# Expert jobs in the order of their experts, one weight load for each expert, and a combine in one-pass matmuls

## The chip, the core and the metric

One NeuronCore of a Trainium2 chip runs one program. Its engines each have a queue of instructions of their own: TensorE (PE in the profile, with its weight loads as PEld), VectorE (DVE), ScalarE (ACT), GpSimd (POOL) and SyncE (SP), which here issues nearly all weight DMAs. Engines wait for one another through semaphores only. The metric is the device time of one execution in microseconds (us). The kernel before takes 1644.32 us (median of three runs, 1644.28 to 1646.38).

## The reference, cut to what matters

Two transformer blocks follow one another on 256 tokens of width 1024. The change touches the mixture of experts at the end of the second (32 experts, 4 chosen for each token, so 1024 assignments), in float32:

```python
logits = (ht @ w_router + b_router).astype(jnp.float32)
top_vals, top_idx = lax.top_k(logits, TOP_K)
gates = jax.nn.softmax(top_vals, axis=-1)
...
def expert_block(args):
    xblk, e = args
    gu = xblk @ w_gate_up[e] + b_gate_up[e]
    gate = jnp.minimum(gu[:, :D_EXPERT], SWIGLU_LIMIT)
    up = jnp.clip(gu[:, D_EXPERT:], -SWIGLU_LIMIT, SWIGLU_LIMIT)
    act = gate * jax.nn.sigmoid(SWIGLU_ALPHA * gate) * (up + 1)
    return act @ w_down[e] + b_down[e]
...
y = jnp.zeros((T + 1, D), h.dtype).at[row_tok].add(row_gate[:, None].astype(h.dtype) * yb)
```

`w_gate_up[e]` is 1024 x 2048 (8 MB), `w_down[e]` 1024 x 1024 (4 MB). With the reference's inputs expert 8 is chosen by 72 tokens and every other expert by 57 or fewer.

## The kernel before

**Jobs.** The experts' work is cut into jobs of up to 64 tokens (`SLOTS`) of one expert. The first 32 jobs are the 32 experts; an expert with more than 64 tokens gets further jobs, which stand behind all others. Here that is one, so there are 33 jobs. VectorE finds the tables of the jobs (expert, token positions, gates) on wide tiles of 16 x 32 numbers (`choose`), beside the first job's matmuls.

**One job on TensorE.** `gather` picks the job's token rows out of `x_n` with a 0/1 matrix `picks` (L1826). `bias` starts the four PSUM banks 0 to 3 (L1836, fp32r, 64 partitions deep: high and low parts of the biases). `gate_up` adds the products with eight weight slots in four pairs (L1849); a pair is 16 matmul instructions with a weight tile of 64 columns each, even chunks into the upper 64 rows of a bank and odd chunks into the lower 64 rows. A float32 matmul of the program is two instructions in the trace, an fp32r matmul or a transposition one. `turn_act` transposes the activation (L1861), `down` multiplies by four weight slots (L1901), `turn_mix` transposes a matrix that holds the gate at each token's slot (L1891), and `combine` spreads the result over the 256 tokens with it (L1873, float32, 64 deep). ScalarE and VectorE fetch the two half sums out of the banks (`lo_rows` and `swap`, L769, L754; L1384, L1357), form the activation on 64 partitions x 1024 (L1390 to L1400), and add the combined rows to `h` (L1376).

**Pipeline.** A turn of the loop holds gate/up of one job (`m + 2`) and, at its end, down of the job before (`m + 1`); combine follows one more turn later. So the activation of a job is made while the next work runs on TensorE.

**Loads.** Twelve slots of 1 MB hold the weights of one job: six of `ring`, six of `ring_b`. SyncE reloads a pair of gate/up slots when TensorE has used it (`gu_used`), and a down slot likewise (`d_used`), for the next job's expert, which it reads from `job_expert`. Every job loads its 12 MB, also the second job of an expert. There is no second set of slots.

## Time and profile before

| | |
|---|---|
| Median of the runs | 1644.32 us |
| The profiled execution's own time | 1646.69 us |
| Its span, first to last instruction | 1644.9 us |
| PE / PEld / DVE / ACT busy | 1540.6 / 859.6 / 674.7 / 383.3 us |
| Mean granted TensorE clock | 0.957 |
| HBM read | 492.36 MB |

The experts' part runs from about 620 us to the end. The profile is read from the page to the windows, and from there to the order of time: the windows say which engines are full, the timeline how long each piece of a turn holds TensorE. A piece's length is taken from the start of one row to the start of the next, since matmul ends overlap.

### The profile page before, as it was taken

How to read it: one execution, taken by the hardware profiler on the slowest of the kernel's cores; microseconds unless marked ns; L12 is line 12 of the kernel's file. 1: busy time of each engine (PE TensorE's matmuls, PEld its weight loads, DVE VectorE, ACT ScalarE, POOL GpSimd, SP SyncE). 2: the span in 40 equal slices, each digit the busy share in tenths (PEclk: the TensorE clock that was granted, in tenths of full speed). 3: DMA queues.
4: the chain of work that ended last, by engine and by line, in shares of the span. 5: the costliest groups of instructions: out<-in, count | busy, mean ns of one | idle time of the engine just before them, and what ended most of it. 6: DMA issues, size and time to landing. Idle time of an engine off the chain costs nothing.

```text
span 1644.9 us, 21236 instructions
## 1 busy us (share of the span) xinstructions
PE 1540.6 (94%) x7730; PEld 859.6 (52%) x7730; DVE 674.7 (41%) x1053; ACT 383.3 (23%) x607; POOL 87.9 (5%) x106
## 2 busy tenths in 40 slices
PE   6999797999968688999999999999999999999995
PEld 5768564899956645344443444444444444344431
DVE  2134424766743425433334334343343343433433
ACT  0222002444312301212213122122131221221212
POOL 2000001322312000000000000000000000000000
PEclk9999797999979787999999999999999999999997
DMA  6332233555523434899999999999999999999993
GB/s 237 132 137 103 102 103 124 169 191 180 170 94 134 179 114 161 328 414 421 422 421 421 421 421 421 421 422 421 422 422 421 421 421 422 422 421 422 421 380 128
DMA packets 106812, 493.82 MB, mean 300 GB/s; under 512 B 10255, under 2 KB 34496, under 8 KB 56032
## 3 DMA queue, kind: packets, MB, share of 16 engines
q1 hardware_dynamic: 103136, 489.85, 74.3%
q10 hardware_dynamic: 3648, 3.59, 0.7%
q8 instruction: 19, 0.31, 0.1%
q14 instruction: 9, 0.07, 0.0%
HBM read 492.36 MB, written 1.05 MB: 300 GB/s over the span
## 4 chain that ended last, share of the span: by engine, by line
issue 64%; PE 31%; DVE 3%; POOL 1%; ACT 1%; DVEq 0%; POOLq 0%; ACTq 0%
PE bank L1480 8%; PE bank L1665 7%; PE bank L1488 6%; PE bank L1677 4%; PE bank L1634 2%; PE bank L1470 1%; PE bank L1777 0%; PE bank L1739 0%; POOL rstd L451 0%; PE bank L1767 0%; DVE u_lo L1119 0%; DVE h_lo L1078 0%; PE bank L1607 0%; PE bank L1544 0%; ACT score L712 0%
## 5 line engine op out<-in xcount | busy, mean ns | idle before, releaser
L1849 PE MATMUL bank<-ring,x_T 128*64 128x512 f32 x1584 | 365.3, 604 | 0.0
L1901 PE MATMUL bank<-ring_b,act_T 128*64 128x512 f32 x1056 | 234.2, 596 | 0.0
L1849 PEld LDWEIGHTS bank<-ring,x_T 128*64 128x64 f32 x1584 | 106.0, 138 | 212.6 <-issue 210.5
L1376 DVE TENSOR_TENSOR h<-h,bank 128x512 f32<-128x512 f32 x128 | 82.2, 684 | 309.3 <-PE bank L1873 296.2
L769 ACT ACTIVATE lo_rows<-bank 64x512 f32<-64x512 f32 x132 | 67.7, 589 | 533.9 <-PE bank L1849 533.9
L1901 PEld LDWEIGHTS bank<-ring_b,act_T 128*64 128x64 f32 x1056 | 73.0, 137 | 137.9 <-issue 137.9
L1826 PEld LDWEIGHTS bank<-picks,x_n 128*128 128x128 f32 x1056 | 123.6, 196 | 27.1 <-issue 27.1
L1384 DVE TENSOR_TENSOR gate<-bank,lo_rows 64x512 f32<-64x512 f32 x66 | 42.3, 678 | 222.9 <-ACT lo_rows L769 222.9
L1826 PE MATMUL bank<-picks,x_n 128*128 128x64 f32 x1056 | 128.2, 281 | 2.3 <-DVE picks L1287 2.3
L1849 PE MATMUL bank<-ring_b,x_T 128*64 128x512 f32 x528 | 120.6, 598 | 0.0
L1480 PE MATMUL bank<-x_nT,ring 128*128 128x256 f32 x512 | 113.8, 385 | 0.8 <-DVE x_nT L878 0.8
L1480 PEld LDWEIGHTS bank<-x_nT,ring 128*128 128x128 f32 x512 | 98.4, 193 | 15.4 <-DVE x_nT L878 1.2
L1665 PE MATMUL bank<-h_hi,ff_hi 128*128 128x256 f32 x352 | 100.5, 285 | 1.9 <-DVE ff_lo L1093 1.9
L1665 PE MATMUL bank<-h_lo,ff_hi 128*128 128x256 f32 x352 | 100.1, 285 | 0.0
L1665 PE MATMUL bank<-h_hi,ff_lo 128*128 128x256 f32 x352 | 100.1, 284 | 0.0
L1357 DVE TENSOR_TENSOR y<-bank,swap 128x512 f32<-128x512 f32 x66 | 45.6, 692 | 80.3 <-ACT swap L755 67.9
L451 POOL TENSOR_TENSOR rstd<-msq,neg_half 128x2 f32<-128x2 f32 (+2 forms) x10 | 8.5, 858 | 1256.7 <-DVE msq L858 1213.4
L1873 PE MATMUL bank<-y,mix_w 64*128 64x512 f32 x248 | 70.0, 641 | 0.0
L1665 PEld LDWEIGHTS bank<-h_hi,ff_hi 128*128 128x128 f32 x352 | 68.2, 194 | 3.4 <-DVE ff_lo L1093 3.0
L1665 PEld LDWEIGHTS bank<-h_lo,ff_hi 128*128 128x128 f32 x352 | 68.2, 194 | 0.4
L1665 PEld LDWEIGHTS bank<-h_hi,ff_lo 128*128 128x128 f32 x352 | 68.1, 193 | 0.0
L1849 PEld LDWEIGHTS bank<-ring_b,x_T 128*64 128x64 f32 x528 | 35.0, 136 | 59.4 <-issue 57.3
(363 smaller groups left out, 1688.8 us busy)
## 6 DMA issues: line engine op xcount, KB each, us to landing
ring<-in_w_gate_up SPq DMA_DIRECT2D x198, 1024.0 KB, 11.4
ring_b<-in_w_down SPq DMA_DIRECT2D x132, 1024.0 KB, 11.3
ring_b<-in_w_gate_up SPq DMA_DIRECT2D x66, 1024.0 KB, 8.4
ring<-in_w_in SPq DMA_DIRECT2D x22, 1024.0 KB, 7.3
ring<-in_w_ffn_in SPq DMA_DIRECT2D x22, 1024.0 KB, 5.1
ring<-in_w_ffn_out SPq DMA_DIRECT2D x11, 1024.0 KB, 4.9
ring<-in_w_out SPq DMA_DIRECT2D x8, 1024.0 KB, 5.4
ring<-in_w_branch_sb SPq DMA_DIRECT2D x2, 1024.0 KB, 5.1
```

Source lines behind the costliest of these rows:

```text
L769: act.activation(t.lo_rows[0:SLOTS, n, :], g.banks[n][SLOTS:, :], ACT.Copy).then_inc(s.lo_rows_ready, 1)
L1357: dve.tensor_tensor(t.y[:, c, :], g.banks[first + c][:], t.swap[:, c, :], ALU.add).then_inc(s.y_summed, 1)
L1376: dve.tensor_tensor(t.h[:, b, cols], t.h[:, b, cols], g.banks[4 + b][:], ALU.add).then_inc(s.added, 1)
L1384: dve.tensor_tensor(dst, g.banks[n][0:SLOTS, :], t.lo_rows[0:SLOTS, n, :], ALU.add).then_inc(s.summed, 1)
L1480: ins = pe.matmul(bank[:, j * T:(j + 1) * T], wk[:, f * P:(f + 1) * P], src[:, k, :], start=(k == 0), stop=(k == len(weights) - 1))
L1488: ins = pe.matmul(bank[:, 0:n], src[:, k, b * P:(b + 1) * P], wk[:, c0:c0 + n], start=(k == 0), stop=(k == len(weights) - 1))
L1665: ins = pe.matmul(bank[:, f * T:(f + 1) * T], wt[:, k, f * P:(f + 1) * P], ht[:, k, :], start=(k == 0 and part == 0), stop=(k == KT - 1 an ...
L1677: ins = pe.matmul(banks[2 * b + c][:], ut[:, q, k, b * P:(b + 1) * P], wt[:, k, 512 * c:512 * c + 512], start=False, stop=last, skip_group ...
L1826: ins = pe.matmul(banks[6][:, f * SLOTS:(f + 1) * SLOTS], t.h_n[:, b, f * P:(f + 1) * P], t.picks[:, b, :], start=(b == 0), stop=(b == 1))
L1849: ins = pe.matmul(banks[n][rows, :], t.x_T[:, c, :], job_slot(g, c)[:, 512 * n:512 * n + 512], start=False, stop=(pair == 3), skip_group_c ...
L1873: ins = pe.matmul(banks[outs + b][:], t.mix_w[rows, b * P:(b + 1) * P], t.y[rows, c, :], start=start, stop=True, skip_group_check=True)
L1901: ins = pe.matmul(banks[outs + n][rows, :], t.act_T[:, 2 * c + i, :], job_slot(g, GU + c)[:, D * i + 512 * n:D * i + 512 * n + 512], start ...
```

## The change

- **Tables.** The jobs are sorted by expert. The number of tokens of each expert comes from a matmul, running sums over experts from matmuls with triangles (`before4`, `upto4`), and the tables of positions, gates and experts from small matmuls with the matrix `job_sel` (job m belongs to expert e).
- **Loads.** SyncE's loop runs over the 31 further experts, not over jobs. It reads `job_last[e]`, the number of the last job of expert e, and reloads a slot when that job has used it.
- **Order.** Gate/up and down of a job stand in one turn. The last pair of gate/up counts bank by bank (`gu_full`). Combine of the job before stands between pairs 1 and 2 and between pairs 2 and 3.
- **Activation.** The two halves of 512 columns lie on the two halves of the partitions, so it is formed on 128 x 512, with the last product written in transposed column order for four 128 x 128 transpositions.
- **Combine.** The gates are no longer in the matrix (`spread` is 0/1); the result is multiplied by the gate (`slot_gate`) and split in a high and a low fp32r part. `bias` and `combine` alternate between the two halves of 64 rows.

```diff
+    sp.wait_ge(s.jobs_ready, 1)
+    with sp.Fori(0, E - 1) as m:
+        last = sp.value_load(t.job_last[0:1, bass.ds(m, 1)], min_val=0, max_val=E + OVER - 1)
         for c in range(GU):
-            if c % 2 == 0:
-                sp.wait_ge(s.gu_used, nth(m, o, 4, c // 2 + 1))
-            load_gu(e, c)
+            pair = c // 2
+            if c % 2 == 0 and pair < PAIRS - 1:
+                sp.wait_ge(s.gu_used, last * (PAIRS - 1) + (pair + 1))
+            elif c % 2 == 0:
+                sp.wait_ge(s.gu_full, last * 4 + 4)
+            load_gu(m + 1, c)
         for c in range(DN):
-            sp.wait_ge(s.d_used, nth(m, o, 4, c - 3))
-            load_down(e, c)
+            sp.wait_ge(s.d_used, last * DN + (c + 1))
+            load_down(m + 1, c)
...
         for n in range(4):
-            ins = pe.matmul(banks[n][:], t.bias_sel[0:64, :], t.bias_hl[0:64, 512 * n:512 * n + 512], start=True,
-                            stop=False, skip_group_check=True)
+            n = n // 2 + 2 * (n % 2)
+            rows, cols = slice(SLOTS * (n // 2), SLOTS * (n // 2) + SLOTS), slice(512 * (n % 2), 512 * (n % 2) + 512)
+            ins = pe.matmul(banks[n][:], t.bias_sel[rows, :], t.bias_hl[rows, cols], start=True, stop=False,
+                            skip_group_check=True)
...
+    def turn_weights(m, o):
+
+        pe.wait_ge(s.mix_in_ready, nth(m, o, 3, 3))
         if m is not None or o > 0:
+            pe.wait_ge(s.act_T_ready, nth(m, o, 1, 0))
+        for b in range(NB):
+            pe.transpose(banks[7][:, b * P:(b + 1) * P], t.mix_in[:, b, :], t.ident[:])
+        for b in range(NB):
+            ins = pe.matmul(banks[7][:, T:T + 1], t.mix_in[:, b, :], t.gate_col[:, b:b + 1], start=(b == 0),
+                            stop=(b == 1))
+        ins.then_inc(s.weights_turned, 1)
...
+        for part in (t.y_hi, t.y_lo):
+            for c in range(2):
+                rows = slice(SLOTS * c, SLOTS * c + SLOTS)
+                ins = pe.matmul(banks[outs + c][:], t.spread[rows, b * P:(b + 1) * P], part[rows, :],
+                                start=(part is t.y_hi), stop=(part is t.y_lo), skip_group_check=True)
         ins.then_inc(s.combined, 1)
...
+    def crossed_gate_up(m, o):
+
         if m is not None or o > 0:
             act.wait_ge(s.summed, nth(m, o, 4, 0))
         for n in range(4):
+            there, here = (slice(SLOTS, P), slice(0, SLOTS)) if n % 2 == 0 else (slice(0, SLOTS), slice(SLOTS, P))
+            act.wait_ge(s.gu_full, nth(m, o, 4, n + 1))
+            act.activation(t.cross[here, n // 2, :], g.banks[n][there, :], ACT.Copy).then_inc(s.crossed, 1)
...
+    next_job(None, 1)
+    add_combined(None, -1)
     swiglu(None, 0)
-    weights(None, 0)
-    next_job(None, 2)
-    add_combined(None, -1)
-    swiglu(None, 1)
```

**TensorE, one turn of the job loop**, in the order of its queue. `y` and `mix_w` belong to combine, `picks` to gather, `act` to turn_act. Before:

```order
561 L1849 MATMUL bank<-ring,x_T 64x512 x8
562 L1855 REGISTER_ALU
563 L1857 REGISTER_ALU
564 L1861 MATMUL bank<-ident,act 128x64 x8
565 L1849 MATMUL bank<-ring,x_T 64x512 x8
566 L1867 ISA
567 L1873 MATMUL bank<-y,mix_w 128x512 x2
568 L1849 MATMUL bank<-ring,x_T 64x512 x8
569 L1870 REGISTER_ALU
570 L1873 MATMUL bank<-y,mix_w 128x512 x2
```

After, from the first combine of the turn to its end:

```order
551 L1860 MATMUL bank<-y_hi,spread 128x512 x2
552 L1860 MATMUL bank<-y_lo,spread 128x512 x2
557 L1842 ISA
558 L1846 MATMUL bank<-ident,mix_in 128x128 x2
559 L1848 MATMUL bank<-gate_col,mix_in 128x1 x2
561 L1825 MATMUL bank<-ring_b,x_T 64x512 x8
562 L1796 ISA
563 L1799 MATMUL bank<-picks,x_n 128x64 x16
564 L1835 REGISTER_ALU
565 L1837 MATMUL bank<-ident,act 128x128 x4
566 L1876 REGISTER_ALU
567 L1882 MATMUL bank<-ring_b,act_T 64x512 x16
```

The transpositions of the activation have moved from behind the next job's first pair to the place right ahead of down of their own job, with only the gather between them and the last gate/up pair. `L1876` is down's wait for the transposed activation.

**TensorE, the first job**, after:

```order
534 L1869 MATMUL bank<-b_down,gate_T 128x512 x2
535 L1825 MATMUL bank<-ring_b,x_T 64x512 x8
536 L1799 MATMUL bank<-picks,x_n 128x64 x16
537 L1869 MATMUL bank<-b_down,gate_T 128x512 x2
538 L1837 MATMUL bank<-ident,act 128x128 x4
539 L1882 MATMUL bank<-ring_b,act_T 64x512 x16
```

Before, the two groups of `b_down` matmuls stood between gate/up pairs of the second job. Now the second of them stands between the first job's last pair and its transpositions, and VectorE's sums of it (`add_combined(None, -1)`) stand ahead of the first job's activation.

## Rows read from the trace of the kernel before

**Rows 1.** The page: chain that ended last by engine; DMA issues of `w_down`.

```profile
issue 64%; PE 31%; DVE 3%; POOL 1%; ACT 1%; DVEq 0%; POOLq 0%; ACTq 0%
...
ring_b<-in_w_down SPq DMA_DIRECT2D x132, 1024.0 KB, 11.3
```

**Rows 2.** Windows: length, busy of PE, PEld, DVE, ACT, POOL, clock, DMA share, GB/s.

```profile
620.00:650.00 30.00, 25.22 (x102) 14.85 (x102) 20.28 (x58) 4.37 (x5) 0.00 (x0) 0.64 0.27 100
...
1000.00:1100.00 100.00, 100.00 (x514) 43.44 (x512) 36.35 (x61) 20.47 (x36) 0.00 (x0) 1.00 1.01 422
```

**Rows 3.** Timeline of PE in one turn: start, length, line, operation, shapes, count.

```profile
1001.01 1.13 PE L1873 MATMUL bank<-y,mix_w 64*128 64x512 f32 x4
1002.07 3.65 PE L1849 MATMUL bank<-ring,x_T 128*64 128x512 f32 x16
...
1006.72 3.79 PE L1826 MATMUL bank<-picks,x_n 128*128 128x64 f32 x32
1010.43 3.65 PE L1849 MATMUL bank<-ring_b,x_T 128*64 128x512 f32 x16
1014.02 0.44 PE L1891 MATMUL bank<-ident,mix_in 128*128 128x128 f32 x2
1014.38 7.09 PE L1901 MATMUL bank<-ring_b,act_T 128*64 128x512 f32 x32
1021.40 1.19 PE L1836 MATMUL bank<-bias_hl,bias_sel 64*128 64x512 f32 x4
1022.53 3.65 PE L1849 MATMUL bank<-ring,x_T 128*64 128x512 f32 x16
1026.11 1.17 PE L1861 MATMUL bank<-ident,act 64*128 64x64 f32 x8
...
1030.80 1.13 PE L1873 MATMUL bank<-y,mix_w 64*128 64x512 f32 x4
```

**Rows 4.** Timeline of PE, float32 matmuls of the full 128 x 128 tile.

```profile
601.41 3.60 PE L1488 MATMUL bank<-ring,y_pool 128*128 128x512 f32 x8
```

**Rows 5.** Timeline of ACT and DVE, the steps of one activation (and its transposed copy).

```profile
1593.14 0.60 ACT L760 ACTIVATE act_T<-bank 128x512 f32<-128x512 f32 x1 [3.28 <-PE bank L1861]
...
1606.10 2.05 ACT L769 ACTIVATE lo_rows<-bank 64x512 f32<-64x512 f32 x4 [12.36 <-PE bank L1849]
...
1606.72 1.28 DVE L1384 TENSOR_TENSOR gate<-bank,lo_rows 64x512 f32<-64x512 f32 x2 [3.00 <-ACT lo_rows L769]
...
1608.04 0.69 DVE L1390 TENSOR_SCALAR gate<-gate 64x1024 f32<-64x1024 f32 x1
...
1610.76 1.22 DVE L1398 SCALAR_TENSOR_TENSOR act<-act,gate 64x1024 f32<-64x1024 f32 x1
```

**Rows 6.** DMA issues (median us to landing): at 780 to 900, at 1500 to 1610, and an FFN load.

```profile
ring<-in_w_gate_up SPq DMA_DIRECT2D x24, 1024.0 KB, 10.7
...
ring<-in_w_gate_up SPq DMA_DIRECT2D x18, 1024.0 KB, 12.7
...
ring<-in_w_ffn_out SPq DMA_DIRECT2D x11, 1024.0 KB, 4.9
```

**Rows 7.** Timeline of DVE and PE from the routing to the first turn of the loop.

```profile
621.83 0.58 DVE L1267 TENSOR_REDUCE mask<-one_hot 128x64 f32<-128x256 f32 x1
...
627.55 7.06 PE L1826 MATMUL bank<-picks,x_n 128*128 128x64 f32 x32 [2.31 <-DVE picks L1287]
...
636.54 12.89 PE L1849 MATMUL bank<-ring,x_T 128*64 128x512 f32 x48
...
660.65 1.20 PE L1836 MATMUL bank<-bias_hl,bias_sel 64*128 64x512 f32 x4 [3.93 <-DVE act L1384]
...
693.82 1.20 PE L1836 MATMUL bank<-bias_hl,bias_sel 64*128 64x512 f32 x4
```

**Rows 8.** Timeline: PE behind the loop's last down, DVE's last additions to `h`.

```profile
1613.38 1.14 PE L1861 MATMUL bank<-ident,act 64*128 64x64 f32 x8
...
1634.39 1.41 DVE L1431 TENSOR_TENSOR h<-h,bank 128x512 f32<-128x512 f32 x2 [0.16 <-DVE h L1431]
```

More of the change, by code:

```diff
@@ L359, in load_down @@
     def load_down(e, c):
[L360 to L363 removed]
+        sp.dma_start(job_slot(g, GU + c), down[e, c // 2, c % 2]).then_inc(s.job_landed(GU + c), 16)
     for c, back in ((0, 6), (1, 5)):
@@ L1883, in down_bias, with down @@
+    def down_bias(b):
+        if b == 1:
+            pe.wait_ge(s.added, 2)
+        for c in range(2):
+            ins = pe.matmul(banks[4 + c][:], t.gate_T[0:E, b * P:(b + 1) * P], t.b_down[0:E, 512 * c:512 * c + 512],
                             start=True, stop=True)
         ins.then_inc(s.combined, 1)
-    def turn_mix(m, o):
-        pe.wait_ge(s.mix_in_ready, nth(m, o, 2, 2))
+    def down(m, o, e):
         pe.wait_ge(s.act_T_ready, nth(m, o, 1, 1))
-        for b in range(NB):
-            ins = pe.transpose(banks[7][:, b * P:(b + 1) * P], t.mix_in[:, b, :], t.ident[:])
-        ins.then_inc(s.weights_turned, 1)
@@ L1925, in tensor_program @@
-    gate_up(None, 1, 3)
-    turn_mix(None, 0)
-    pe.wait_ge(s.added, 2 * NB)
-    down(None, 0, 4)
-    def job_turn(m, final=False):
-        bias(m, 2)
-        gate_up(m, 2, 0)
-        turn_act(m, 1)
-        gate_up(m, 2, 1)
-        combine(m, 0, 0, 4)
-        gate_up(m, 2, 2)
-        combine(m, 0, 1, 4)
-        if not final:
-            gather(m, 3)
-        gate_up(m, 2, 3)
-        turn_mix(m, 1)
-        pe.wait_ge(s.added, nth(m, 1, 4, 4))
-        down(m, 1, 4)
-    pe.wait_ge(s.jobs_ready, 1)
@@ L1947, in tensor_program @@
-    more = pe.value_load(t.job_count[0:1, 0:1], min_val=E - 3, max_val=E + OVER - 3)
+    pe.wait_ge(s.over_ready, 1)
+    for n, sums in enumerate((t.before4, t.upto4)):
+        ins = pe.matmul(banks[5][:, n:n + 1], sums[0:E, :], t.over[0:E, :], start=True, stop=True)
+    ins.then_inc(s.starts_made, 1)
+    pe.wait_ge(s.bias_ready, 2)
+    bias(None, 0)
+    gate_up(None, 0, 0, 0)
+    bank = open_bank(r2, "gT")
+    pe.wait_ge(s.gates_ready, 1)
+    for b in range(NB):
+        ins = pe.transpose(bank[0:E, b * P:(b + 1) * P], t.gate_e[:, b, :], t.ident[:])
@@ new lines, in tensor_program @@
+    ins.then_inc(s.filled2, 1)
+    gate_up(None, 0, 0, 1)
+    pe.wait_ge(s.sel_ready, 1)
+    pe.wait_ge(s.pos_T_ready, 1)
+    pe.wait_ge(*r2.drained("gT"))
+    for b in range(NB):
+        toks, pos, gate = (slice(c0, c0 + n) for c0, n in ((b * P, P), (b * JOBS, JOBS), (128 + b * JOBS, JOBS)))
+        pe.matmul(banks[4][:, pos], t.pos_T[0:E, toks], t.job_sel[0:E, :], start=True, stop=False)
+        pe.matmul(banks[4][:, pos], t.back[0:E, :], t.block[0:E, :], start=False, stop=True)
+        pe.matmul(banks[4][:, gate], t.gate_T[0:E, toks], t.job_sel[0:E, :], start=True, stop=True)
@@ new lines, in tensor_program @@
+    pe.matmul(banks[4][0:1, 256:256 + JOBS], t.part32[0:E, :], t.job_sel[0:E, :], start=True, stop=True)
+    pe.matmul(banks[4][0:1, 320:320 + E], t.span[0:E, 1:2], t.ident[0:E, 0:E], start=True,
+              stop=True).then_inc(s.tables_made, 1)
+    turn_weights(None, 0)
+    gate_up(None, 0, 0, 2)
+    pe.wait_ge(s.b_down_in, 16)
+    pe.wait_ge(s.jobs_ready, 1)
+    down_bias(0)
+    gate_up(None, 0, 0, 3)
+    gather(None, 1)
+    down_bias(1)
+    turn_act(None, 0)
+    down(None, 0, 0)
@@ new lines, in job_turn @@
+    def job_turn(m, final=False):
+        e = pe.value_load(t.job_expert[0:1, bass.ds(m + 1, 1)], min_val=0, max_val=E - 1)
+        bias(m, 1)
+        gate_up(m, 1, e, 0)
+        gate_up(m, 1, e, 1)
+        combine(m, 0, 0)
+        gate_up(m, 1, e, 2)
+        combine(m, 0, 1)
+        turn_weights(m, 1)
+        gate_up(m, 1, e, 3)
+        if not final:
+            gather(m, 2)
+        turn_act(m, 1)
+        down(m, 1, e)
+    more = pe.value_load(t.job_count[0:1, 0:1], min_val=E - 2, max_val=E + OVER - 2)
```

490 lines of the change are left out of this document (224 added, 266 removed).

## The prediction, made before the changed kernel ran

> **What bounds the kernel now.** I read the page first. Its chain of what ended last calls 64% of the span "issue", time in which TensorE waited for nothing that the profile shows, so the experts' part is one unbroken stream of matmuls [rows 1]. The windows confirm it: in 1000 to 1100 us PE is busy for 100.00 of 100 us at a granted clock of 1.00 (the 2.4 GHz level). They show a second thing: the DMA engines are full as well (share 1.01, 422 GB/s) [rows 2]. Both resources are at their end and only one can set the pace. A turn takes 1030.80 - 1001.01 = 29.79 us on PE [rows 3]. The 12 MB of a job (12.58 million bytes) at 421 to 422 GB/s take 29.85, call it 29.87. The time to landing decides: a load lands 10.7 us after its issue early in the loop and 12.7 late in it [rows 6]. The queue grows very slowly, by under 0.1 us a turn, and a landed slot still waits over 10 us for its use. So PE sets the pace, and DMA stands 0.3% behind it. There are 132 / 4 = 33 jobs [rows 1].
>
> **A turn, piece by piece.** By starts in [rows 3]: combine 1.06, twice; a gate/up pair 3.59, four times; gather 3.71; turn_mix 0.36; down 7.02; bias 1.13; turn_act takes what is left of 29.79, 1.10. Down has 32 instructions and a pair 16: 16 more cost 3.43, so 0.16 of each stretch is the change from one form of weight tile to another (for that, the Trainium skill, TensorEngine Tiling (Array Packing), "Key Properties", says that a change of mode drains the engine; the trace agrees, and what it costs here is the 0.16).
>
> - **Bias and combine.** Four bias instructions cost 1.13 - 0.16 = 0.97, 0.24 each, one after another in the same rows. The two float32 matmuls of a combine are four instructions in 1.06 although one alone takes 0.43 (8 in 3.60 [rows 4]): the two halves of rows run side by side. After, bias and combine are four one-pass instructions each that alternate between the halves. Taken side by side: 2 x 0.24 + 0.16 = 0.64. No row shows fp32r in alternating halves, so the bounds are 0.64 and 1.13 (the bias row as it is); I take 0.64, since the halves are what the combine row shows to be shared. Saved: 0.49 and 2 x 0.42.
> - **Gate/up** is unchanged, 4 x 3.59, less one change of form between pairs 0 and 1: 14.20.
> - **turn_weights** is turn_mix plus two matmuls of one column, four instructions that each load 128 weight columns; a gather instruction, which is bound by that load, costs (3.71 - 0.16) / 32 = 0.11. So 0.36 + 0.44 = 0.80.
> - **Gather** 3.55, without the change of form at its end.
> - **turn_act and the wait behind it.** Four transpositions at 0.12 to 0.16 each (bounded by turn_act's 8 in 1.10 and turn_mix's 2 in 0.36), about 0.6 with the drain. Then down needs `act_T`, which ScalarE copies in 0.60 [rows 5]; with two hand-overs of 0.05 and its being behind the copy of `x_T`, PE stands still for about 0.8. Before, this copy was hidden behind a gate/up pair. Together 1.4.
> - **Down** 7.02. A read of `job_expert` is added at the head of each turn; the read of `job_count` before the first turn left down at its full pace and cost nothing visible, and I take 0.
>
> Sum: 0.64 + 1.28 + 14.20 + 0.80 + 3.55 + 1.4 + 7.02 = **28.9 us** a turn (28.8 to 29.3), against 29.79.
>
> **The wait that is added.** The transpositions wait for the activation of the same job. Behind the last gate/up pair only the gather, 3.55, covers it. From the start of that pair: banks 0 to 3 are full at about 1.07, 1.92, 2.78 and 3.64. ScalarE's copies take 0.59, VectorE's additions 0.64 to 0.68, a limit on 128 x 512 half of 0.69 plus overhead, 0.43, a product half of 1.22 plus overhead, 0.67 [rows 5]. The additions end at 2.4, 3.3, 4.35 and 5.0, the second limit at 5.5, the two products at 6.2 and 6.9. PE would reach the transpositions at 3.59 + 3.55 = 7.14. The chain fits with 0.2 to spare: cover is thin, and each 0.1 more on that chain beyond it costs 3 us over 32 turns. The sum over `h`, the new split in high and low part and the job's tables lie beside gate/up: from the end of down they need about 3.4 us, and combine comes 7.7 us later.
>
> **Loads after.** They would be 32 x 12 MB, but the saved load does not shorten DMA by its 29.9 us: during expert 8's first job no slot is given back, DMA runs empty, and it starts again in job 9. From there it is always full: 23 experts at 29.87. The first pair is free 4.2 us into job 9's turn. The second-last pair of the last expert lands 22 x 29.87 + 6 x 2.49 + 2.4 later (2.4 is the 4.9 us of an unqueued load [rows 6] less its 2.49 of transfer), 678.6 us after job 9's start, and 20.7 us of the turn remain: 699.3. PE alone needs 24 x 28.9 = 693.6. So DMA takes over shortly before the end, and the part from job 9 on takes 699 for every turn below 29.14. This is a floor; the first nine jobs are PE's.
>
> **Before the loop** [rows 7]. The mask is there at 622.4; the rank matmuls no longer wait for the gates, so gather starts at about 625.1 instead of 627.55. It takes 7.06 as now, the clock in this stretch being granted at 0.64 on average [rows 2], two small matmuls 0.9, bias 1.2: the first pair at 634.2 instead of 636.54. It costs 5.9 with the slow clock. Then 0.4 (gates turned), 3.6, tables 2.1 (16 instructions at 0.11 and changes of form), 0.8, 3.6, `b_down` 1.9, 3.6, gather 3.7, `b_down` 1.9: 661.7. Here VectorE begins the two last additions of `b_down` and only then the activation: 1.4 + 2.6 + 0.9 + 1.4 = 6.4 with PE idle, twice the 3.93 that [rows 7] shows now. After that gap the clock falls again, as it did at 660.65; transpositions and copy 1.8, down 9. The loop starts with job 1 at **679**, against 693.82 with job 2. So 32 turns remain instead of 31.
>
> **The end.** Job 9 starts at 679 + 8 x 28.9 = 910.2, and the last down ends 699.3 later, plus 1.8 for a slow clock in the last turn, where no gather covers the activation: 1611.3. Before, it is 1613.38 [rows 8]; there a second down and two more combines follow, and the last addition to `h` ends at 1635.80, 9.1 before the end. Now there follow half sums and split 3.4, combine about 0.9, additions 2.8: 7.1, and the same 9.1. Span 1611.3 + 16.2 = **1627.5**, 17.4 less than 1644.9. The profiled execution took 1646.69 where the median is 1644.32; I take the difference from the median and get **1627 us**, 1.05% faster.
>
> **Rivals.**
> - **The halves do not run side by side in fp32r.** Then bias and both combines stay at 1.13 and a turn is 28.9 + 3 x 0.49 = 30.4. 32 turns from 679 end at 1651, the span at 1669: **1668 us**, slower. It speaks for it that no row shows it, against it that the float32 combine does it in the same tiles. The point of decision is a piece length of about 0.9. By TensorE: Matmul & The Clock Gate, Part 3, of the Trainium skill, a weight load overlaps running matmuls only in other rows, and combine loads its low part's weights under the high part: that would give the same lengthening by another way. The bias row, at 0.24 per one-pass instruction in the same rows, speaks against it.
> - **The activation outlasts the gather.** If the hand-overs or the product with strided output take 0.5 to 1.0 more in all, a turn is 29.2 to 29.7: span 1637 to 1653, typically **1643**.
> - **Loads slower.** `w_down` is now read in pieces of 8 KB at twice the distance. If those four of twelve loads take 5% more, an expert takes 30.4 and the floor from job 9 rises by 11: **1638**.
> - **The part before the loop is better hidden** (clock stays up, no gap of 6.4): 5 less, **1621**.
>
> **How the numbers follow.** Forecast 1619 to 1636: 0.62. Activation longer 0.16; loads slower 0.07; halves one after another 0.08; still faster 0.07. A difference of about 0.2% (3.3 us) is what a measurement can tell from none. Faster by more holds the forecast, the last, and most of the two middle ones: 0.80. Within 0.2%: 0.07. Slower 0.13, mostly the first rival. The range leaves out that rival and the tails: 1616 to 1650.
>
> **What would show it.** In the profile after: starts of a turn 28.9 apart before job 9; bias and combine pieces near 0.64, or 1.13 if the first rival holds; one gap of PE of 0.8 a turn before down, released by ScalarE's `act_T`, and none before the transpositions; DMA below full in job 8's turn, then full, with landing times growing by about 1 us a turn, and PE waiting for slots only in the last turns; a gap of 6 us before the first job's transpositions. I am wrong if a turn is not within 28.7 to 29.3, or if waits for loads appear early.

## The result, and the profile after

The changed kernel takes 1648.35 us (median of 15 runs, 1645.69 to 1652.40), the kernel before beside it 1644.35 us (15 runs, 1642.03 to 1648.43). The ratio is 1.0021, with a 95% interval of 1.0011 to 1.0031. The forecast was 1627 us. So the change that was to save 17 us costs 4. The profiled execution of after took 1650.08 us, its span is 1648.3 us, its mean granted TensorE clock 0.950, PE was busy for 1504.2 us (1540.6 before), and 479.77 MB were read (492.36 before). TensorE has 36 us less work and ends later.

Here is the same view as [rows 3], TensorE in one turn of the loop: start, length, line, operation, count, and in brackets the idle time ahead and what ended it.

```profile
705.29 0.74 PE L1812 MATMUL bank<-bias_hl,bias_sel 64*128 64x512 f32 x4
705.96 7.09 PE L1825 MATMUL bank<-ring,x_T 128*64 128x512 f32 x32
712.98 0.50 PE L1860 MATMUL bank<-y_hi,spread 64*128 64x512 f32 x2
...
713.64 3.65 PE L1825 MATMUL bank<-ring,x_T 128*64 128x512 f32 x16
717.23 0.50 PE L1860 MATMUL bank<-y_hi,spread 64*128 64x512 f32 x2
...
717.89 0.44 PE L1846 MATMUL bank<-ident,mix_in 128*128 128x128 f32 x2
...
718.60 3.65 PE L1825 MATMUL bank<-ring_b,x_T 128*64 128x512 f32 x16
722.18 3.79 PE L1799 MATMUL bank<-picks,x_n 128*128 128x64 f32 x32
726.20 0.65 PE L1837 MATMUL bank<-ident,act 128*128 128x128 f32 x4 [0.24 <-DVE act L1376]
727.73 7.09 PE L1882 MATMUL bank<-ring_b,act_T 128*64 128x512 f32 x32 [0.88 <-ACT act_T L781]
734.75 0.74 PE L1812 MATMUL bank<-bias_hl,bias_sel 64*128 64x512 f32 x4
```

This turn takes 734.75 - 705.29 = 29.46 us, 0.33 less than before and 0.57 more than forecast. Bias takes 0.67 and each combine 0.66: those gains are there. But TensorE now stands still twice in every turn, 0.24 us ahead of the transpositions (waiting for VectorE's `act`) and 0.88 us ahead of down (waiting for ScalarE's `act_T`). In [rows 3] it never did.

VectorE on the activation of that job, to be held beside [rows 5], and ScalarE's copy of `act_T` behind the transpositions:

```profile
722.39 1.41 DVE L1360 TENSOR_TENSOR up<-bank,cross 64x512 f32<-64x512 f32 x2
723.83 0.43 DVE L1371 TENSOR_SCALAR up<-up 128x512 f32<-128x512 f32 x1
724.29 0.69 DVE L1373 TENSOR_TENSOR gate<-gate,sig 128x512 f32<-128x512 f32 x1
725.02 1.05 DVE L1376 SCALAR_TENSOR_TENSOR act<-up,gate 128x512 f32<-128x512 f32 x1
...
726.89 0.60 ACT L781 ACTIVATE act_T<-bank 128x512 f32<-128x512 f32 x1 [0.29 <-PE bank L1837]
```

The last product, written in transposed column order, takes 1.05 us where the product of the same shape above it takes 0.69. The chain ends at 726.07, 7.47 us after the last pair's start at 718.60.

The second finding is not in the usual turn but in every fourth. The windows (length, busy time of PE, PEld, DVE, ACT, POOL, granted clock, DMA share, GB/s) at the end of such a turn, where down starts at 875.00:

```profile
871.00:875.00 4.00, 2.89 (x25) 2.54 (x24) 2.24 (x4) 1.19 (x2) 0.00 (x0) 1.00 1.01 422
875.00:878.40 3.40, 3.40 (x8) 1.15 (x10) 0.00 (x0) 0.00 (x0) 0.00 (x0) 0.50 1.02 424
878.40:882.00 3.60, 3.60 (x20) 1.43 (x18) 0.00 (x0) 0.00 (x0) 0.00 (x0) 1.00 1.01 419
```

TensorE came out of the gather, two idle stretches and four transpositions (2.89 us busy of 4.00). For the first part of down the granted clock is then 0.50, the 1.2 GHz level: 8 matmuls in 3.40 us, against 20 in the 3.60 behind it. Such a turn takes 31.12 us instead of 29.45. There are seven of them among the 31 turns from 675.83 to 1600.53, always four turns (119.5 us) apart, and an eighth fall comes in the last turn's down. The kernel before had none in this part; its window from 700 to 1590 us:

```profile
700.00:1590.00 890.00, 890.00 (x4484) 376.17 (x4482) 336.22 (x565) 204.46 (x360) 0.00 (x0) 1.00 1.01 421
```

The loads, from the page (issues, KB each, median us to landing), beside [rows 1, 6]:

```profile
ring<-in_w_gate_up SPq DMA_DIRECT2D x192, 1024.0 KB, 9.6
ring_b<-in_w_down SPq DMA_DIRECT2D x128, 1024.0 KB, 8.2
```

A `w_down` load lands sooner than before (11.3), and no PE instruction in the loop waits for a load. The windows of the trace show DMA at a share of 1.01 up to 890 us, at 0.00 from 895 to 915 us, and at 1.00 again from 920 us on: it rests once, in expert 8's first job, as foreseen.

**The account.** From the start of job 1 to the end of the last down the forecast gave 932.3 us; after takes 1631.55 - 675.83 = 955.7. Of the 23.4 in between, 31 turns at 29.45 instead of 28.9 make 17.1, the seven falls 7 x 1.67 = 11.7, the last turn (31.0 where 28.9 and 1.8 were counted) 0.3; against this, the 5.7 us by which the loads were to hold back a faster TensorE at the end did not come. The loop starts 3.2 earlier than forecast, the tail is 0.5 longer (16.75 against 16.2): 23.4 - 3.2 + 0.5 = 20.7, and the span is 20.8 above 1627.5.

### The profile page after: what moved, and what is told of

The parts are those of the page before. It is cut to its first block, busy times and chain, and to the rows that moved or that the text cites. A ratio compares the mean times of both kernels' runs of the same rounds, so it can differ in the third digit from the quotient of the medians.

```text
span 1648.3 us, 21328 instructions
## 1 busy us (share of the span) xinstructions
PE 1504.2 (91%) x7752; PEld 861.7 (52%) x7753; DVE 659.7 (40%) x1103; ACT 372.9 (23%) x608; POOL 89.9 (5%) x117
## 3 DMA queue, kind: packets, MB, share of 16 engines
HBM read 479.77 MB, written 1.05 MB: 292 GB/s over the span
## 4 chain that ended last, share of the span: by engine, by line
issue 64%; PE 31%; DVE 3%; POOL 1%; ACT 1%; DVEq 0%; POOLq 0%; ACTq 0%
PE bank L1456 8%; PE bank L1641 7%; PE bank L1464 6%; PE bank L1653 4%; PE bank L1610 2%; PE bank L1446 1%; PE bank L1753 0%; PE bank L1715 0%; POOL rstd L434 0%; PE bank L1743 0%; DVE u_lo L1104 0%; DVE h_lo L1063 0%; PE bank L1583 0%; PE bank L1588 0%; PE bank L1520 0%
## 5 line engine op out<-in xcount | busy, mean ns | idle before, releaser
L1825 PE MATMUL bank<-ring,x_T 128*64 128x512 f32 x1584 | 356.5, 599 | 0.0
L1882 PE MATMUL bank<-ring_b,act_T 128*64 128x512 f32 x1056 | 248.3, 624 | 28.7 <-ACT act_T L781 28.7
L1319 DVE TENSOR_TENSOR y_sum<-bank,y_cross 64x512 f32<-64x512 f32 x66 | 45.5, 689 | 328.9 <-ACT y_cross L740 327.8
L1882 PEld LDWEIGHTS bank<-ring_b,act_T 128*64 128x64 f32 x1056 | 88.7, 144 | 167.3 <-issue 166.2
L1456 PEld LDWEIGHTS bank<-x_nT,ring 128*128 128x128 f32 x512 | 96.9, 190 | 14.8 <-DVE x_nT L863 1.1
L754 ACT ACTIVATE spread<-bank 128x256 fp32r<-128x256 f32 x33 | 12.6, 383 | 353.9 <-PE bank L1848 333.6
L764 ACT ACTIVATE cross<-bank 64x512 f32<-64x512 f32 x132 | 78.0, 591 | 41.5 <-PE bank L1825 41.4
L740 ACT ACTIVATE y_cross<-bank 64x512 f32<-64x512 f32 x33 | 19.6, 594 | 260.0 <-PE bank L1882 260.0
```

Of the source, the lines that this page charges most:

```text
L740: act.activation(t.y_cross[0:SLOTS, :], g.banks[4][SLOTS:, :], ACT.Copy).then_inc(s.y_crossed, 1)
L764: act.activation(t.cross[here, n // 2, :], g.banks[n][there, :], ACT.Copy).then_inc(s.crossed, 1)
L1319: dve.tensor_tensor(t.y_sum[rows, :], g.banks[4 + c][rows, :], t.y_cross[rows, :], ALU.add).then_inc(s.y_summed, 1)
L1456: ins = pe.matmul(bank[:, j * T:(j + 1) * T], wk[:, f * P:(f + 1) * P], src[:, k, :], start=(k == 0), stop=(k == len(weights) - 1))
L1825: ins = pe.matmul(banks[n][rows, :], t.x_T[:, c, :], job_slot(g, c)[:, 512 * n:512 * n + 512], start=False, stop=(pair == PAIRS - 1), skip ...
L1882: ins = pe.matmul(banks[4 + n][rows, :], t.act_T[:, k, SLOTS * (c // 2):SLOTS * (c // 2) + SLOTS], job_slot(g, GU + c)[:, D * i + 512 * n: ...
```

## The experiments

Each kernel is the changed kernel with the edit shown, unless another is named. They were timed beside the kernel before, whose median was 1644.09 (first four), 1644.0 (next four) and 1642.25 us (last four). The ratios are those recorded against the runs of the kernel before in the same session; they can differ by 0.15% from the quotient of the two medians.

### Which part of the excess is the chain

**e1_contiguous.**

```diff
-        dve.scalar_tensor_tensor(out=t.act[:].rearrange("s (k p) -> s p k", k=4),
-                                 in0=up[:].rearrange("s (p k) -> s p k", k=4), scalar=1.0,
-                                 in1=gate[:].rearrange("s (p k) -> s p k", k=4), op0=ALU.add,
-                                 op1=ALU.mult).then_inc(s.act_ready, 1)
+        dve.scalar_tensor_tensor(out=t.act[:], in0=up[:], scalar=1.0, in1=gate[:], op0=ALU.add,
+                                 op1=ALU.mult).then_inc(s.act_ready, 1)
...
-            ins = pe.transpose(banks[7][:, k * P:(k + 1) * P], t.act[:, k * P:(k + 1) * P], t.ident[:])
+            ins = pe.transpose(banks[7][:, k * P:(k + 1) * P], t.act[:, k:512:4], t.ident[:])
```

> The last product of the activation is written in its natural order (as before the change), and the transpositions read every fourth column. Theory A (TensorE sets the pace; turns of 29.46 us, of which every fourth is 1.67 longer because the clock falls to 1.2 GHz at the start of down): the product goes from 1.05 to about 0.67 us, the wait of 0.24 before the transpositions disappears, a usual turn is 29.22; about 7 us less in all, if the falls of the clock stay as often. Theory B (the loads set the pace: the mean turn of 29.83 equals 29.87, the time of 12 MB): the turn's pieces shorten in the same way, but the mean turn stays at 29.8 and the total within 2 us of the changed kernel.

Measured: 1630.99 us (1627.78 to 1632.16), ratio 0.9922 (0.9900 to 0.9943): 17 us below after, where theory A gave 7 with the falls left in, and no longer slower than before but 0.8% faster. The timeline of one turn, with the steps of TensorE and VectorE in it:

```profile
1011.37 3.79 PE L1797 MATMUL bank<-picks,x_n 128*128 128x64 f32 x32
...
1014.21 0.69 DVE L1376 SCALAR_TENSOR_TENSOR act<-up,gate 128x512 f32<-128x512 f32 x1
...
1015.03 0.74 PE L1835 MATMUL bank<-ident,act 128*128 128x128 f32 x4
...
1016.65 0.65 PE L1880 MATMUL bank<-ring_b,act_T 128*64 128x512 f32 x2 [0.88 <-ACT act_T L781]
```

The product takes 0.69 us, there is no idle time before the transpositions (3.66 from the gather's start, 4.02 in after), and the strided read costs TensorE 0.09 on the four transpositions. The turn is 29.19 us. The clock does not fall in any turn of the loop. So one edit, of the order in which one product is written and read, removes both the 0.27 a turn and the falls in the loop.

(Of the strided write, the Trainium skill, SBUF — State Buffer, "Door 1: The DMA port swizzle", says that each access that crosses to a new line of 16 bytes pays a penalty; it gives no size. The 1.05 against 0.69 agrees with it in direction.)

**e2_filler.**

```diff
         turn_act(m, 1)
+        pe.wait_ge(s.summed, nth(m, 1, 4, 4))
+        for n in range(FILL):
+            pe.matmul(banks[n][:], t.bias_sel[:, :], t.bias_hl[:, 0:512], start=True, stop=True,
+                      skip_group_check=True)
         down(m, 1, e)
```

with `FILL = 3`.

> Three useless one-pass matmuls of 512 columns stand between the transpositions and down, where TensorE waits 0.88 us for act_T; nothing is read from what they write. Theory A: they take 0.7 of time in which nothing ran, so a usual turn stays at 29.46, but the clock no longer falls in the loop: 8 x 1.67 = 13 us less than the changed kernel, 1635, and landing times of the loads grow over the loop (29.46 against 29.87). Theory B: no change, 1648, TensorE then waits for slots. Third theory (the clock falls because of the gather and the transpositions, not because of the gap): falls stay, 1648.

Measured: 1633.53 us (1629.45 to 1635.50), ratio 0.9931 (0.9909 to 0.9953). Three matmuls that nobody needs make the kernel 15 us faster than after:

```profile
1020.94 0.65 PE L1838 MATMUL bank<-ident,act 128*128 128x128 f32 x4 [0.24 <-DVE act L1377]
1021.35 0.95 PE L1940 MATMUL bank<-bias_hl,bias_sel 128*128 128x512 f32 x3
1022.28 7.09 PE L1883 MATMUL bank<-ring_b,act_T 128*64 128x512 f32 x32
```

The wait for `act` is still there, the wait for `act_T` is filled. No fall of the clock in the loop, and down starts 1.34 us after the start of the transpositions instead of 1.53. The turn is 29.27, where I had written 29.46. The gather and the transpositions stand as in after, so the third theory is out. This separates the falls from the chain: the chain is as long as in after, and what has changed is what TensorE does behind the transpositions.

**e11_fill_one** is the same with one matmul, `FILL = 1`.

> As e2_filler with one useless 128x512 matmul instead of three between the transpositions and the first matmul of down; its result is overwritten by the next bias. It ends about 0.6 us before act_T is there, so down still starts from standstill and the usual turn stays 29.45 us. Theory A (total idle time of a turn decides on the falls; 1.12 us before, 0.88 us now, and e1_contiguous with 0.88 us had none): no falls of the clock in the loop, 1633 to 1637 us. Theory B (a stretch without any wait before down is what prevents them): falls every 4th turn as before, 1646 to 1650 us.

Measured: 1631.36 us (1630.14 to 1635.32), ratio 0.9932 (0.9909 to 0.9954); the median is below my range, the ratio is that of e2_filler.

```profile
723.79 0.47 PE L1940 MATMUL bank<-bias_hl,bias_sel 128*128 128x512 f32 x1
724.08 0.60 ACT L782 ACTIVATE act_T<-bank 128x512 f32<-128x512 f32 x1 [0.29 <-PE bank L1838]
724.73 7.09 PE L1883 MATMUL bank<-ring_b,act_T 128*64 128x512 f32 x32 [0.46 <-ACT act_T L782]
```

One matmul is enough against the falls, with 0.46 us of wait left ahead of down. I was wrong on the turn: it is 29.26, not 29.45, since down starts 1.34 us after the transpositions (at 723.39) here too. Down's first matmul follows the end of ScalarE's copy by 0.24 us in after (727.49 to 727.73) and by 0.05 here (724.68 to 724.73). Whether the shorter stand does it, or that another instruction than a transposition stands ahead, no run tells.

### Is it the length of the chain or the strided access

**e9_contig_reclamp** is e1_contiguous with the chain made as long again by other means; `JOB_DVE_STEPS` becomes 3.

```diff
         own(dve.tensor_scalar(up[:], up[:], SWIGLU_LIMIT, -SWIGLU_LIMIT, ALU.min, ALU.max))
+        own(dve.tensor_scalar(up[:, 0:384], up[:, 0:384], SWIGLU_LIMIT, -SWIGLU_LIMIT, ALU.min, ALU.max))
```

> The product is written in natural order as in e1_contiguous (0.69 us instead of 1.05), but `up` is clamped a second time on 384 of its 512 columns ahead of it (about 0.35 us, changes no value), so that the activation chain is as long as in the changed kernel. Theory A (it is the length of the chain against the gather that costs, whatever makes it long): TensorE idle again about 0.25 us before the transpositions and 0.88 us behind them, usual turns 29.45 us, a fall of the clock about every 4th turn, 1645 to 1650 us. Theory C (the strided product itself does harm, by its accesses): turns 29.2 us, no falls, 1629 to 1633 us as e1_contiguous.

Measured: 1647.27 us (1643.66 to 1652.10), ratio 1.0025 (1.0011 to 1.0039). Nearly the whole gain of e1_contiguous is gone, so it was the length and not the access.

```profile
730.39 0.74 PE L1836 MATMUL bank<-ident,act 128*128 128x128 f32 x4 [0.27 <-DVE act L1377]
732.01 7.09 PE L1881 MATMUL bank<-ring_b,act_T 128*64 128x512 f32 x32 [0.88 <-ACT act_T L781]
```

But the parts differ from what I expected. The usual turn is 29.58 (the longer strided transpositions come on top of the wait), and the profiled execution has three falls in the loop, not seven, at 761, 1000 and 1031 us. It has slightly more idle time in a turn than after (1.15 against 1.12) and fewer falls. That execution is the slowest of the ten (1652.10 us); no other was traced.

**e10_reclamp** is after with a second clamp of all 512 columns.

> The changed kernel with a second clamp of `up` on all 512 columns (0.43 us and 0.03 to the next, changes no value), so that the chain is 0.46 us longer. Theory A (idle time in every turn makes the clock fall): TensorE idle 0.70 us before the transpositions, usual turns 29.91 us (14.7 us over all), and the falls come more often than every 4th turn: every 3rd gives 4 us more, every 2nd 13 us: 1667 to 1676 us. Theory D (the falls keep their own distance of about 119.5 us, whatever the idle time): 1663 us.

Measured: 1679.11 us (1677.06 to 1680.24), ratio 1.0214 (1.0194 to 1.0234), 31 us above after for 0.46 us of VectorE's time in a turn. The timeline at the transpositions and down of one turn, and a window at the start of another turn's down (columns as above):

```profile
728.26 0.65 PE L1838 MATMUL bank<-ident,act 128*128 128x128 f32 x4 [0.69 <-DVE act L1377]
729.79 8.46 PE L1883 MATMUL bank<-ring_b,act_T 128*64 128x512 f32 x32 [0.88 <-ACT act_T L781]
```

```profile
790.70:794.00 3.30, 3.02 (x8) 1.11 (x10) 0.00 (x0) 0.04 (x1) 0.00 (x0) 0.50 1.00 417
```

The usual turn is 29.91 as computed, and the clock falls in every second turn (31.53 us), in 16 of 31, with one pair of falls in neighbouring turns. So theory D, falls at a fixed distance of their own, is out, and more idle time at this place brought more falls. The 31 us are 14.7 from the chain, nine more falls at 1.62 for 14.6, and about 2 in the first job. The upper end of my range, 1676, was 3 us short.

### The gap before down

**e3_bias_in_gap** moves the next job's bias, which needs nothing of this one, to the place where TensorE waits for `act_T` (in the first job likewise).

```diff
-        bias(m, 1)
         gate_up(m, 1, e, 0)
...
         turn_act(m, 1)
+        if not final:
+            bias(m, 2)
         down(m, 1, e)
```

> The next job's bias matmuls (0.66 a turn) stand between the transpositions and down instead of at the head of the next turn. Theory A: they fill the gap, a usual turn is 28.8, and the clock falls no more; then DMA becomes the bound some turns after job 9 and the total is 1624 to 1630 against 1648. If the clock keeps falling every fourth turn: 13 us more, about 1638. Theory B: 1646 to 1648.

Measured: 1623.99 us (1622.32 to 1628.23), ratio 0.9878 (0.9860 to 0.9896). The timeline of TensorE in an early turn, from its transpositions to its down, and two pairs of a late one, and the window of the late turns:

```profile
726.93 0.65 PE L1837 MATMUL bank<-ident,act 128*128 128x128 f32 x4 [0.24 <-DVE act L1376]
727.51 0.73 PE L1812 MATMUL bank<-bias_hl,bias_sel 64*128 64x512 f32 x4
728.27 7.09 PE L1882 MATMUL bank<-ring_b,act_T 128*64 128x512 f32 x32
...
1282.05 3.65 PE L1825 MATMUL bank<-ring,x_T 128*64 128x512 f32 x16 [0.42 <-DMA ring<-in_w_gate_up]
...
1287.02 3.65 PE L1825 MATMUL bank<-ring,x_T 128*64 128x512 f32 x16 [0.65 <-DMA ring<-in_w_gate_up]
```

```profile
1211.00:1585.00 374.00, 357.64 (x1875) 157.58 (x1872) 135.33 (x259) 80.96 (x148) 0.00 (x0) 1.00 1.01 422
```

The turn is 28.45 us until about 1211 us (I had written 28.8: down also starts 0.19 sooner behind the transpositions, as in e2_filler), and no clock falls in it. From there TensorE waits for its loads in every turn, 1.07 us in the one shown, and a turn takes 29.83, the time of 12 MB. Here the floor of the prediction is seen at work. The late turns show one thing more. By the window TensorE stands for 374.00 - 357.64 = 16.4 us in 12.5 turns, 1.3 us a turn, more than the 1.12 of after, and the clock stayed at 1.00. These waits lie between long rows of gate/up matmuls, and only 0.24 us of them ahead of the transpositions. So it is not the sum of idle time in a turn that brings the falls.

### Are the loads the pace of after

A mean turn of after is (1600.53 - 675.83) / 31 = 29.83 us, the very time that DMA needs for 12 MB. That looks like a kernel bound by its loads.

**e4_half_loads.** From expert 1 on only the first half of each slot is loaded.

```diff
-            load_gu(m + 1, c)
+            sp.dma_start(job_slot(g, c)[:, 0:CW // 2],
+                         gate_up[m + 1, c][:, 0:CW // 2]).then_inc(s.job_landed(c), 16)
```

and likewise for `w_down`.

> From the second expert on only the first half of every weight slot is loaded (the other half keeps the first expert's numbers), so DMA needs half of its time; all matmuls stay. Theory A: the same time as the changed kernel, 1648, the same turns of 29.46 with every fourth 31.1. Theory B: the turns fall to TensorE's own work, all of them 29.46, and the total to about 1635.

Measured: 1651.72 us (1650.20 to 1652.69), ratio 1.0047 (1.0029 to 1.0064). A load lands after 4.3 to 4.7 us, and the turns are the same: 29.45, and the same seven of them 31.1. Half the traffic, no gain. The equality of 29.83 was a coincidence.

**e6_load_per_job** gives SyncE back its loop over jobs, with 33 loads. TensorE then waits for the load of its job's number, and no longer reads `job_expert`; everything else is after.

```diff
-    with sp.Fori(0, E - 1) as m:
-        last = sp.value_load(t.job_last[0:1, bass.ds(m, 1)], min_val=0, max_val=E + OVER - 1)
+    more = sp.value_load(t.job_count[0:1, 0:1], min_val=E - 2, max_val=E + OVER - 2)
+    def next_loads(m):
+        e = sp.value_load(t.job_expert[0:1, bass.ds(m + 1, 1)], min_val=0, max_val=E - 1)
```

> The changed kernel, but with the weights loaded once for each job again (33 loads of 12 MB, the second job of expert 8 loads its own). Theory A: the saved load is worth nothing here, because DMA is not the bound and the saved load only makes DMA idle: 1646 to 1650, the same turns. Rival: the saved 12 MB are worth their transfer time: 1678.

Measured: 1650.07 us (1647.69 to 1650.30), ratio 1.0040 (1.0025 to 1.0055), within 2 us of after, with the same turns. The saved load, 12.6 MB, is worth nothing measurable while TensorE sets the pace.

### The first job

**e7_first_job** lets VectorE form the first job's activation before the second addition of `b_down`'s rows.

```diff
-    add_combined(None, -1)
+    add_combined(None, -1, (0,))
     swiglu(None, 0)
+    add_combined(None, -1, (1,))
```

> Only the third repair: in the first job VectorE forms the activation before it adds the second b_down part. Theory A: TensorE's gap of 6.86 us before the first transpositions shrinks to under 0.5; 6 to 8 us less than the changed kernel (the clock doesn't fall there either), 1640 to 1643, and the falls of the clock every fourth turn stay.

Measured: 1648.22 us (1645.81 to 1652.73), ratio 1.0036 (1.0024 to 1.0049). A miss: nothing gained. The timelines around the first job's transpositions, first of after, then of e7_first_job:

```profile
658.85 1.28 DVE L1351 TENSOR_TENSOR h<-h,bank 128x512 f32<-128x512 f32 x2 [7.92 <-PE bank L1869]
658.91 0.38 ACT L754 ACTIVATE spread<-bank 128x256 fp32r<-128x256 f32 x1 [20.38 <-PE bank L1869]
...
659.38 2.44 ACT L764 ACTIVATE cross<-bank 64x512 f32<-64x512 f32 x4
660.05 1.40 DVE L1360 TENSOR_TENSOR gate<-bank,cross 64x512 f32<-64x512 f32 x2
...
665.67 1.11 PE L1837 MATMUL bank<-ident,act 128*128 128x128 f32 x4 [6.86 <-DVE act L1376]
667.47 8.43 PE L1882 MATMUL bank<-ring_b,act_T 128*64 128x512 f32 x32 [0.69 <-ACT act_T L781]
```

```profile
656.09 0.38 ACT L754 ACTIVATE spread<-bank 128x256 fp32r<-128x256 f32 x1 [20.37 <-PE bank L1870]
...
657.19 1.41 DVE L1360 TENSOR_TENSOR gate<-bank,cross 64x512 f32<-64x512 f32 x2 [9.08 <-ACT cross L764]
...
662.81 0.47 PE L1838 MATMUL bank<-ident,act 128*128 128x128 f32 x1 [6.81 <-DVE act L1376]
```

From the start of `spread` to the first addition of `gate` it is 1.14 us in after and 1.10 in e7. VectorE's additions to `h` had lain beside ScalarE's copy of `spread` and its first `cross`. Both engines were released by the same last matmul of `b_down`, and by the order of the queues either one is enough to hold the chain: VectorE's additions end at 660.13 in after, and ScalarE's first crossed half is there at about the same time. ScalarE waits for that matmul ahead of `spread`, and the four copies of crossed halves are queued behind that, so to move VectorE's additions alone gains nothing. The gap is 6.81 instead of 6.86.

**e5_three_repairs** is e1_contiguous, e3_bias_in_gap and e7_first_job in one.

> The product in natural order (as in e1), the next job's bias in the gap (as in e3), and in the first job VectorE adds the second b_down part after the activation instead of ahead of it. Theory A: the gap of 6.86 us before the first transpositions goes, so job 1 starts 6 us sooner than in e3; turns of 28.2 until DMA is the bound (from about job 19 on 29.83); from the start of job 9 to the last down 704, as in e3, which no shorter turn can change. Median 1616 to 1620, against 1624 for e3. If DMA were no floor: 28.2 throughout, about 1595.

Measured: 1620.92 us (1619.96 to 1624.49), ratio 0.9868 (0.9847 to 0.9888), 1 us above my range. The third repair gave nothing (TensorE still stands for 6.47 us before the first transpositions); of the 3 us below e3_bias_in_gap, about 2 are the shorter turns ahead of job 9, seven at 28.18 instead of 28.45. A turn is 28.18 us until 1146 us, then 29.82 with waits for loads (17.4 us in 26 waits from 1180 to 1560, 1.4 a turn), none of it beside the transpositions, and no fall.

**e8_repairs_load_per_job** is e5_three_repairs with 33 loads, by the edit of e6_load_per_job.

> e5 with one load for each job (33 loads). Theory A: now TensorE's turns are shorter than the loads, so the rest that DMA's queue gets during expert 8's first job counts: without it DMA is the bound from about job 11 on, some 13 us more than e5, about 1631. Rival (one load for each expert is worth nothing in any case): the same as e5.

Measured: 1635.69 us (1632.23 to 1637.98), ratio 0.9946 (0.9927 to 0.9965), 14.8 us above e5, where 13 were forecast. TensorE waits for loads from 921 us on. Beside e6 this is the point on the saved load: worth 15 us with TensorE at 28.2 a turn, and nothing at 29.45 with a fall in every fourth.

**e12_first_job** is e5_three_repairs with one edit more, in ScalarE's program:

```diff
         act.wait_ge(s.weights_turned, nth(m, o, 1, 1))
-        act.wait_ge(s.combined, nth(m, o, 2, 2))
+        if m is not None or o > 0:
+            act.wait_ge(s.combined, nth(m, o, 2, 2))
         act.activation(t.spread[:], g.banks[7][:, 0:T], ACT.Copy).then_inc(s.mix_ready, 1)
```

> e5_three_repairs, and in the first job ScalarE no longer waits for the second addition of down's bias before it copies the spread weights (nothing has read them yet), behind which its copies of the crossed halves and so the whole activation chain of the first job were queued. Theory A (this queue position is what made e7_first_job a miss): TensorE's idle time before the first transpositions shrinks from 6.5 us to under 0.5 us, everything behind it moves forward by 6 us, since the loads rest anyway in expert 8's first job: 1612 to 1617 us. Rival (one more wait of the same length stands behind it, or the loads at the end give the gain back): 1619 to 1622 us as e5_three_repairs.

Measured: 1613.15 us (1610.69 to 1613.91), ratio 0.9808 (0.9789 to 0.9827), 1.9% faster than before and the fastest of all. The timeline of TensorE in the first job, and the window from the start of job 9's first pair to the end of the last down:

```profile
654.58 3.79 PE L1799 MATMUL bank<-picks,x_n 128*128 128x64 f32 x32
658.30 1.98 PE L1869 MATMUL bank<-b_down,gate_T 32*128 32x512 f32 x4
660.21 0.75 PE L1837 MATMUL bank<-ident,act 128*128 128x128 f32 x4
660.89 0.74 PE L1812 MATMUL bank<-bias_hl,bias_sel 64*128 64x512 f32 x4
661.70 7.09 PE L1882 MATMUL bank<-ring_b,act_T 128*64 128x512 f32 x32
```

```profile
895.40:1595.40 700.00, 677.14 (x3566) 300.40 (x3562) 255.66 (x501) 156.30 (x287) 0.00 (x0) 1.00 0.99 413
```

The gap is gone, and with it the clock's fall in the first down (7.09 us instead of the 8.43 of after). From the start of the first job's gather to the loop's first pair it is 14.0 us instead of the 22.6 of e5; 6.5 of these 8.6 us are the gap, the rest is the slow clock behind it. The medians of e5 and e12, of two sessions, differ by 7.8 us. ScalarE's wait alone, with VectorE's additions left where they were, was not tried. From job 9 on the kernel takes 700.0 us, TensorE busy for 677.14 of them; the rest is waiting for loads and the last turn's gaps.

## Why the prediction was wrong

**What bounds the kernel now: right.** TensorE set the pace before and after. e4_half_loads and e6_load_per_job show it for after.

**The turn and the total.** The turn came out at 29.46, beyond the 28.7 to 29.3 that the prediction had set itself as the sign of being wrong. The total of 1648 us lies within the stated 1616 to 1650 only because that range was wide: the forecast of the span missed by 20.7 us and in the wrong direction, and falls of the clock for which the reasoning had no place added 11.7. That the time lies in the range is luck.

**Bias, combine, gate/up, down: right.** Forecast 0.64, 1.28, 14.20 and 7.02; by starts they measured 0.67, 1.32, 14.19 and 7.02. turn_weights took 0.71 where 0.80 was taken, and the read of `job_expert` cost nothing (without it, in e6_load_per_job, the turn is 29.45 as well). Halves in alternation do run side by side in fp32r, so the rival that was to make the kernel slower is refuted, by either of its two ways. The rows of [rows 3] and [rows 4] had been enough for this.

**The wait that is added: wrong, and this is the step that failed.** "The chain fits with 0.2 to spare" rested on a product of 0.67 on 128 x 512, half of the 1.22 of [rows 5] plus overhead. That row was contiguous; the diff's product is not. It took 1.05, and the additions ended 0.2 later than the 5.0 summed. So the chain ended 7.47 us after the last pair's start, against 6.9 forecast, and 0.13 more pass before the transpositions start, at 7.60. In e1_contiguous, where they need not wait, they start 3.66 us after the gather, 7.24 after the pair. So where 0.2 was to spare, 0.36 were lacking (the trace shows 0.24 of them as idle, since the gather's modelled end overlaps). The row for the strided write did not exist, and I gave it a value instead of bounds. The prediction named the price itself (0.1 beyond the cover costs 3 us), and named this as a rival, "the activation outlasts the gather", at 29.2 to 29.7 a turn and 1643 us, with a chance of 0.16 only. That rival came, with 29.45; its 1643 us had no falls of the clock in them. With a margin of 0.2 us on a chain of some ten instructions, that case should have had about as much weight as the forecast.

**turn_act and the wait behind it: 1.4 against 1.53.** The prediction gave each hand-over 0.05; from the end of ScalarE's copy to down it is 0.24 in after, and 0.05 only in kernels with a matmul in the gap (e2_filler, e3_bias_in_gap, e11_fill_one). Of the 0.57 us by which the turn exceeds 28.89, 0.47 stand between the starts of gather and transpositions (0.36 the chain, 0.11 the gather itself, 3.66 for 3.55) and 0.13 here; the other pieces nearly cancel.

**The clock: wrong, and it follows from the same step.** The prediction counts a slow clock in the first job and, with 1.8, in the last turn, and nothing for the turns between, without a reason; its 0.8 us of idle time in every turn were taken to be harmless. By themselves they are: e1_contiguous has 0.88 and no fall in the loop. Together with 0.24 ahead of the transpositions they brought seven falls in the loop, 11.7 us. Without these after would be at about 1636 to 1637, an estimate from 1648.35 - 11.7, faster than before. So the size of the chain alone would not have turned the sign; the falls that came with it did. In the kernel before the granted clock was 1.00 throughout this part and TensorE never stood there; no row of it could show what 1.1 us in a turn do, and I had no rival for it. (The Trainium skill, TensorE: Matmul & The Clock Gate, "A second HAM failure mode: psum-queue depth-cycling", tells of a kernel in which short idle stretches between groups of matmuls were enough to make the clock go down and up. The trace agrees, with 0.24 and 0.88 us at the place where it falls; the late turns of e3_bias_in_gap, with 1.3 us elsewhere, show that not every such stretch does it.)

**Loads after: right as a mechanism, and hidden.** One rest in expert 8's first job, then full: so it is. The floor of 699.3 from job 9 on, with 1.8 for the slow clock, was not reached by after, whose turns are too long. e12_first_job reaches it, at 700.0 with the last turn's slow clock in it, against 701.1.

**Before the loop: near in size, half of the cause.** The gap before the first transpositions is 6.86 us where 6.4 was written (its terms add up to 6.3, and that is 1.6 times the 3.93 of before, not twice). VectorE's additions are not all of it: e7_first_job moved them and gained nothing, and only when e12_first_job took away ScalarE's wait as well did the gap go. The loop started 3.2 us earlier than forecast, but 1.9 of these lie ahead of the first job's gather, which starts anywhere from 620.3 to 625.8 us in the traces of after, e4_half_loads and e7_first_job, with the same program up to there; so that is scatter, not a test. The tail, 16.75 against 16.2, was right.

**What stays open.** Which turns have a fall, and why. Idle time beside the transpositions goes with its presence: none in the loop with 0.88 (e1_contiguous) or 0.24 and 0.46 us (e11_fill_one), some with 1.12 (after), many with 1.57 (e10_reclamp). The sum over the turn does not: the late turns of e3_bias_in_gap and e5_three_repairs stand for 1.3 and 1.4 us, nearly all of it for loads, and have none. Nor does idle time explain the number: e9_contig_reclamp had three falls with 1.15 where after had seven. In the traces of after, e4_half_loads, e6_load_per_job and e7_first_job the falls come in the same seven turns, the 7th, 11th and so on, though the loop starts at 673.0 to 678.4 us in them. The length of the turn may count too; that was not tried. Each kernel has one trace, so how the falls differ between executions of one kernel is not shown.

## What to carry to other kernels

When a change turns a hidden chain into one that a single piece of work covers, count the chain instruction by instruction, and price each access pattern that no row shows from both sides. If the margin is smaller than that uncertainty, the case "it doesn't fit" is as likely as the forecast. A short wait in every turn can cost twice: once as itself, and once more by a clock that falls behind it; work put into the gap took the falls away (here even a useless matmul), and real work that had to be done anyway (the next job's bias) shortened the turn as well. And before an engine's work is moved, look for every engine that waits for the same event: one that is left keeps the chain where it was.

## What the runs showed of the hardware

- A product on 128 x 512 float32 on VectorE takes 0.69 us, with its output written at a stride of 512 bytes 1.05 us. Four transpositions that read at a stride of four elements instead of contiguously cost TensorE 0.09 us more.
- With 1.12 us of idle time in a turn of 29.5 us, in two pieces around four transpositions and behind a gather of small matmuls, the granted clock went to the 1.2 GHz level for 3.4 us in every fourth turn, at 1.67 us each; with 1.57 us at the same place in every second; with 0.88, behind the transpositions alone, in none. With 1.3 to 1.4 us a turn of waits for loads between long rows of matmuls it did not fall (e3_bias_in_gap, e5_three_repairs).
- One useless 128 x 512 matmul in the gap (e11_fill_one) took about 15 us off the kernel's time by the ratios (0.9932 against 1.0021), three (e2_filler) as much.
- Four one-pass fp32r matmuls, 64 rows deep and 512 columns wide, take 0.67 us when they alternate between the two halves of rows, and 1.13 in the same half (the bias of after and of before).
- Down starts 1.34 us after the start of the transpositions when TensorE had a matmul in between, and 1.53 us when it had none.
